# Two-layer hybrid block plus recurrent and pooling block: the SBUF offsets of the dense products' operands are changed

## The chip, the cores and the metric

The kernel runs on one core of a Trainium2 chip. The metric is the device time of one launch in microseconds (us). SBUF, the on-chip memory, has 128 partitions; a tile's "offset" below is the byte at which it begins within each partition.

## The reference

Two blocks are computed one behind the other on an activation of 512 tokens by 1024 features, in float32.

```python
for l in range(2):                       # first block, 2 layers
    h = x @ w_in[l]                      # 1024 -> 768 + 352 + 1792 columns
    mix = concat(stick_breaking(h), latent_attention(h), rwkv7(h)) @ w_o[l]
    x = layer_norm(ALPHA * x + mix)
    u_act, u_gate = split(x @ ffn_w_up[l])            # 1024 -> 2 * 2816
    hid = gelu(causal_conv3(u_act)) * u_gate
    x = layer_norm(ALPHA * x + hid @ ffn_w_down[l])   # 2816 -> 1024
for i in range(2):                       # second block: one recurrent, one pooling layer
    x = x + gate_m * mixer_i(modulate(rms_norm(x)))
    u = relu(modulate(rms_norm(x)) @ ffn_w1[i])       # 1024 -> 4096
    x = x + gate_f * ((u * u) @ ffn_w2[i])            # 4096 -> 1024
return rms_norm(x)
```

## The kernel before

Features lie on the partitions and the 512 tokens along a partition: x is [128, 8, 512], eight feature tiles of 512 floats (2048 bytes) each. A dense product is built from chunks of the weights, 128x8x128 floats (512 KB), that are streamed from HBM in the order of use. One chunk gives one output tile of 128 features by 512 tokens in one of two PSUM banks (dense0, dense1), from eight 128x128 weight blocks.

The precision of float32 is kept by splitting both operands into a high and a low part in the type float32r, which TensorE takes in one go. ScalarE copies a landed chunk of `raw` to its high part `wh` (L1345), VectorE subtracts to get the low part `wl` (L1959), and each weight block then costs three matmuls: high weights by high activations (L581), high weights by low activations (L582), low weights by high activations (L583). In all three the weight block is the stationary operand, loaded by LDWEIGHTS, and the activation tile of 512 columns is the moving one, streamed by MATMUL. A row of the trace names the moving tile first: `dense<-xh,wh` streams xh against wh.

```python
pe.matmul(o, a, h, start=first, stop=False)          # L581: wh, activation high
pe.matmul(o, a, l, start=False, stop=False)          # L582: wh, activation low
return pe.matmul(o, b, h, start=False, stop=last)    # L583: wl, activation high
```

The activation's two parts are xh and xl for the products that read x (the input, mixer, output and up projections), and hidh and hidl for the down projections of both blocks and for the recurrent layer's block-diagonal products. ScalarE writes hidh (L1684), VectorE writes hidl (L1991). The small low-rank products of the first block read the pairs latent_h/latent_l and lora_in_h/lora_in_l in the same three matmuls. In the pooling layer (L1250 to L1252) the roles are turned: the weights are moving, 256 columns of them, and xh, xl or a single column of shift_h/shift_l, repeated 128 times, is stationary; the values of the latent attention (L790 to L792) are made in the same way with latent_h and latent_l stationary. All else on TensorE is ordinary float32.

The order of work on each engine is written out by hand; SyncE (SP) issues the loads of `raw` in two slots of one chunk each, as the slots come free. The engines wait for one another by semaphores: TensorE for `lo_done` (the chunk's wl is there), for `bank_free`, and for the semaphores of its activation tiles; ScalarE's L1345 waits until TensorE is through with the chunk that was in the slot (`pe_chunk`).

SBUF is laid out by hand as well. `sb` and `Region` place one tile behind the other and round each size up to 32 bytes; the first tile begins at a multiple of 64 bytes. Everything up to and with `cst` therefore begins at a multiple of 64 bytes. The size of cst is 7944 bytes, which is rounded to 7968, and with it most of what comes behind begins 32 bytes past a multiple of 64.

Of the kernel before, what the change touches and what calls it, by code (L numbers as in the profile page):

```python
# [18 lines left out]
F32 = mybir.dt.float32  # L19
F32R = mybir.dt.float32r  # L20
# [6 lines left out]
P = 128  # L27
S = 512
D = 1024
KT = D // P  # L30
CHUNK = KT * P
BLOCKS = S // P
# [9 lines left out]
DECAY = float(np.exp(-0.5))  # L42
LN_EPS, RMS_EPS, GN_EPS = 1e-5, 1e-6, 64e-5
NEG = -1e30


C_MLA, C_SB, C_WAG = 0, 3, 9
# [84 lines left out]
VC, NVC = columns(CONSTS)  # L132
# [84 lines left out]
def build(nc, x_in, stream, mod_stream, vecs1, vecs2, consts, bands, c_rows, out):  # L217
    ctx = ExitStack()
    with ctx:

        top = [nc.sbuf_usable_end - nc.sbuf_bytes_remaining + 63]
        top[0] -= top[0] % 64
        limit = nc.sbuf_usable_end

        def at(name, shape, offset, dt=F32):
            size = 4 * int(np.prod(shape[1:]))
            assert offset + size <= limit, (name, offset, size, limit)
            return nc.alloc_sbuf_tensor_at(name, shape, dt, offset=offset)

        def sb(name, shape, dt=F32):  # L230
            t = at(name, shape, top[0], dt)
            top[0] += (4 * int(np.prod(shape[1:])) + 31) // 32 * 32
            return t

        x = sb("x", [P, KT, S])
        xh_at = top[0]
        xh = sb("xh", [P, KT, S], F32R)
        xl_at = top[0]
        xl = sb("xl", [P, KT, S], F32R)
        raw = sb("raw", [P, 2, CHUNK])  # L240
        wh = sb("wh", [P, 2, KT, P], F32R)
        wl = sb("wl", [P, 2, KT, P], F32R)
        cst = sb("cst", [P, NVC])
        pv_next = sb("pv_next", [P, NV1])
        pv = sb("pv", [P, NV1])
        one_minus = sb("one_minus", [P, 14 + 4])
        pv2 = sb("pv2", [P, NV2])
        cond = sb("cond", [P, D])
        mod = sb("mod", [P, DEPTH, 48])
        small = sb("small", [P, 16, 8])  # L250
# [16 lines left out]
        r0 = top[0]  # L267

        class Region:
# [2 lines left out]

            def __call__(self, name, shape, dt=F32):
                t = at(name, shape, self.at, dt)
                self.at += (4 * int(np.prod(shape[1:])) + 31) // 32 * 32
                return t


        rg = Region(front_at)
# [7 lines left out]
        rg = Region(r0)  # L287
# [11 lines left out]
        rg = Region(at0)  # L299
# [9 lines left out]
        rg = Region(wts_end)  # L309
# [16 lines left out]
        rg = Region(vsb_at)  # L326
# [15 lines left out]
        yy = hats[:, 1]  # L342

        rg = Region(r0)
        hidh = rg("hidh", [P, 8, S], F32R)
        hidl = rg("hidl", [P, 8, S], F32R)
        hf = rg("hf", [P, 2, S])
        ua = rg("ua", [P, S + 4])
# [7 lines left out]
        gate = at("gate", [P, 8, S], front_at)  # L356
        xc = rg("xc", [P, 8, S])
        gx_upper = rg("gx_upper", [P, 4, S])
        tb_last = rg("tb_last", [P, S])
        gx_lower = at("gx_lower", [P, 4, S], mraw_at)  # L360
        ga_lower = at("ga_lower", [P, 6, S], krv_at + 16384)
        ga_upper = at("ga_upper", [P, 2, S], krv_at + 8192)
        shift_h = rg("shift_h", [P, 8], F32R)
        shift_l = rg("shift_l", [P, 8], F32R)
        band = at("band", [P, 8, P + 16], front_at)
        z_tok = at("z_tok", [P, 4, BLOCKS, 256], r0)
        z_shift = at("z_shift", [P, 4, 256], r0 + 16384)


        ga = [ga_lower[:, m, :] for m in range(6)] + [ga_upper[:, m, :] for m in range(2)]  # L370
# [204 lines left out]
        def _(pe):  # L575
            def split_product(o, w, w_rows, k_rhs, first, last):

                (slot, cols), (h, l) = w, k_rhs
                a = wh[w_rows, slot].rearrange("p k m -> p (k m)")[:, cols:cols + P]
                b = wl[w_rows, slot].rearrange("p k m -> p (k m)")[:, cols:cols + P]  # L580
                pe.matmul(o, a, h, start=first, stop=False)  # L581
                pe.matmul(o, a, l, start=False, stop=False)  # L582
                return pe.matmul(o, b, h, start=False, stop=last)  # L583
# [196 lines left out]
            def latent_up(L, pl):  # L780

                s0, s1 = C_UP % 2, (C_UP + 1) % 2
                pe.wait_ge(lo_done, pl.chunk(C_UP) + 1)
                pe.wait_ge(cl_ready, L * 3 + 3)
                ukv_h = wh[:, s0].rearrange("p k m -> p (k m)")[:, 768:1024]
                ukv_l = wl[:, s0].rearrange("p k m -> p (k m)")[:, 768:1024]
                for tb in range(BLOCKS):
                    o = aux[tb // 2][:, 256 * (tb % 2):256 * (tb % 2) + 256]
                    th, tl = ch[:, 2, tb * P:(tb + 1) * P], cl[:, 2, tb * P:(tb + 1) * P]
                    pe.matmul(o, th, ukv_h, start=True, stop=False)  # L790
                    pe.matmul(o, th, ukv_l, start=False, stop=False)
                    m = pe.matmul(o, tl, ukv_h, start=False, stop=True)  # L792
                    if tb % 2:
                        m.then_inc(vup_pe, 1)
                for p in range(2):
                    split_product(aux[4 + p][:], (s0, 512 + p * P), slice(0, P),
                                  (ch[:, 2, :], cl[:, 2, :]), True, True).then_inc(up_pe, 1)
                for h in UP_HEADS:
                    if h == 2:
                        pe.wait_ge(vtok_ready, L * 2 + 2)  # L800
                    if h < 2:
                        pe.wait_ge(vmla_ready, L * 2 + h + 1)
                    m = split_product(aux[h][:], (s0, h * P), slice(0, P),
                                      (ch[:, 0, :], cl[:, 0, :]), True, False)
                m.then_inc(pe_chunk, 1)
                pe.wait_ge(lo_done, pl.chunk(C_UP + 1) + 1)
                for h in UP_HEADS:
                    m = split_product(aux[h][:], (s1, h * P), slice(0, 64),
                                      (ch[0:64, 1, :], cl[0:64, 1, :]), False, True)
                    m.then_inc(up_pe if h != UP_HEADS[-1] else pe_chunk, 1)  # L810
# [393 lines left out]
            for h in range(4):  # L1204
                pe.wait_ge(lo_done, pl.chunk(C_AX + h) + 1)
                pe.wait_ge(hidl_ready, H0 + 2 * h + 2)
                for o in range(4):
# [3 lines left out]
                    for k in range(2):  # L1211
                        m = split_product(aux[n % 6][:], (h % 2, (2 * o + k) * P), slice(0, P),
                                          (hidh[:, 2 * h + k, :], hidl[:, 2 * h + k, :]),
                                          k == 0, k == 1)
# [26 lines left out]

            def pool_weights(w, g, k):

                return w[:, g // 2].rearrange("p k m -> p (k m)")[
                    :, 512 * (g % 2) + 256 * k:512 * (g % 2) + 256 * k + 256]

            def token_rows(o, h, l, g, k):
# [88 lines left out]
        def _(act):  # L1336
            chain = Chain(act, act_chain)

            def prepare(pl, s, i=0, lead=False):

                slot = s % 2
                act.wait_ge(w_landed[slot], pl.landed(s, i))
                if not lead:
                    act.wait_ge(pe_chunk, pl.chunk(s, i) - 1)
                act.activation(wh[:, slot].rearrange("p k m -> p (k m)"), raw[:, slot, :],  # L1345
                               ACT.Copy).then_inc(hi_done, 1)

            def done(pl, s, i=0, more=True):
# [6 lines left out]
            def early(pl, s, q):  # L1355


                for j in range(2):
                    act.wait_ge(w_landed[j], pl.landed(s + j, 1))
                    act.wait_ge(pe_half, 2 * q + j + 1)  # L1360
                    act.activation(wh[:, j, 0:4].rearrange("p k m -> p (k m)"),
                                   raw[:, j, 0:4 * P], ACT.Copy).then_inc(hi_half, 1)

            def rest(pl, s):

                slot = s % 2
                act.wait_ge(pe_chunk, pl.chunk(s) + 1)
                act.activation(wh[:, slot, 4:8].rearrange("p k m -> p (k m)"),
                               raw[:, slot, 4 * P:8 * P], ACT.Copy).then_inc(hi_done, 1)

            def square(k, m):
# [496 lines left out]
            for i in range(4):  # L1868
                for j in range(2):
                    m = i * 2 + j  # L1870
# [80 lines left out]
        def _(dve):  # L1951
            chain = Chain(dve, dve_chain)
            tt, stt, ts = dve.tensor_tensor, dve.scalar_tensor_tensor, dve.tensor_scalar
            MUL, ADD, SUB = ALU.mult, ALU.add, ALU.subtract

            def prepare(n, slot):

                dve.wait_ge(hi_done, n + 1)
                tt(wl[:, slot].rearrange("p k m -> p (k m)"), raw[:, slot, :],  # L1959
                   wh[:, slot].rearrange("p k m -> p (k m)").bitcast(F32), SUB)\  # L1960
                    .then_inc(lo_done, 1)

            def done(pl, s, i=0, more=True):
# [5 lines left out]
            def early(q):  # L1969


                for j in range(2):
                    dve.wait_ge(hi_half, 2 * q + j + 1)
                    tt(wl[:, j, 0:4].rearrange("p k m -> p (k m)"), raw[:, j, 0:4 * P],
                       wh[:, j, 0:4].rearrange("p k m -> p (k m)").bitcast(F32), SUB)\
                        .then_inc(lo_half, 1)

            def rest(pl, s):

                slot = s % 2  # L1980
                dve.wait_ge(hi_done, pl.chunk(s, 1) + 1)
                tt(wl[:, slot, 4:8].rearrange("p k m -> p (k m)"), raw[:, slot, 4 * P:8 * P],
                   wh[:, slot, 4:8].rearrange("p k m -> p (k m)").bitcast(F32), SUB)\
                    .then_inc(lo_done, 1)

            def refill(pl, s, i=0, more=True):
# [434 lines left out]
            for L in range(DEPTH):  # L2421
# [8 lines left out]
                for a in range(4):  # L2430
                    for e in range(2):
# [4 lines left out]
                        m = 2 * a + e  # L2436
# [12 lines left out]
                for g, tiles in enumerate(GROUPS1):  # L2449
# [17 lines left out]
                    for i in range(tiles):  # L2467
                        t = L * 22 + 8 * g + i
                        m = i + 8 * g
# [131 lines left out]
            for i in range(4):  # L2601
                for j in range(2):
                    m = i * 2 + j
# [382 lines left out]
```

## Time and profile before

| | us |
|---|---|
| median of 3 runs | 2461.92 |
| lowest and highest | 2461.33, 2462.2 |
| span of the profiled execution, first to last instruction | 2460.3 |
| TensorE busy in it | 2385.6 |

The profile gives the profiled execution's span; the runs' times lie 1.0 to 1.9 us above it, which is what lies around the span. In a row of the page, busy time is in us and the mean duration of one instruction in ns. TensorE's matmuls are pipelined: one starts before the one ahead of it has ended. So the cost of one in a stream is the distance from its start to the next one's start, and not its duration, and the rows of the timeline give that distance.

### The profile page before, as it was taken

Reading aid. Unit: us, or ns where it says so; the run is one execution under the profiler, and the core shown is the slowest. Engines: PE = TensorE matmul, PEld = TensorE weight load, DVE = VectorE, ACT = ScalarE, POOL = GpSimd, SP = SyncE. Lnnn points to the kernel's source line nnn. Section 1 sums busy time; section 2 is a strip of 40 time slices with the busy share of each in tenths; the row PEclk is TensorE's granted clock in tenths of the full one; section 3 lists DMA queues with packets and bytes.
Section 4 is the critical chain, followed back from the end, with each engine's and each line's share of the span. In section 5 each row is a group of like instructions: output and inputs, shape, how many; then the busy total and the mean of one; then the engine's idle time right before and its main releaser. Section 6 shows DMA issues by size and latency. Waiting matters only on the chain.

```text
span 2460.3 us, 35763 instructions
## 1 busy us (share of the span) xinstructions
PE 2385.6 (97%) x13448; PEld 1890.4 (77%) x13448; DVE 1378.6 (56%) x1936; ACT 982.1 (40%) x1507; POOL 242.1 (10%) x192
## 2 busy tenths in 40 slices
PE   8999999999999999999999999999999999999998
PEld 6766767888887765777888887777888888788886
DVE  4547767656545447857656546575443345533443
ACT  5535435333235535534323234564232233422332
POOL 0041210000022032311000012101000001000001
PEclk9999999999999999999999998999999999999999
DMA  4210014555432210003555431222222222222222
GB/s 157 86 60 18 19 52 147 191 192 188 140 108 70 86 65 30 19 29 137 195 188 189 155 101 57 89 77 96 94 96 97 97 94 69 78 97 97 97 94 85
DMA packets 68796, 248.33 MB, mean 101 GB/s; under 512 B 7632, under 2 KB 8144, under 8 KB 68688
## 3 DMA queue, kind: packets, MB, share of 16 engines
q1 hardware_dynamic: 68688, 246.85, 29.8%
q8 instruction: 72, 1.18, 0.2%
q14 instruction: 36, 0.29, 0.0%
HBM read 244.72 MB, written 2.10 MB: 100 GB/s over the span
## 4 chain that ended last, share of the span: by engine, by line
PE 86%; DVE 7%; ACT 4%; issue 2%; DMA 0%; POOL 0%; DVEq 0%; SPq 0%; ACTq 0%; POOLq 0%
PE dense L581 24%; PE dense L583 24%; PE dense L582 24%; PE aux L688 2%; PE aux L875 1%; PE aux L845 1%; PE aux L862 1%; ACT wh L1345 1%; PE aux L953 1%; PE aux L964 1%; PE aux L1049 1%; DVE wl L1959 1%; PE aux L695 1%; PE dense L609 1%; PE aux L849 0%
## 5 line engine op out<-in xcount | busy, mean ns | idle before, releaser
L581 PE MATMUL dense<-xh,wh 128*128 128x512 f32 x1840 | 733.6, 399 | 24.7 <-DVE wl L1959 10.6
L1345 ACT ACTIVATE wh<-raw 128x1024 fp32r<-128x1024 f32 x346 | 366.9, 1060 | 960.7 <-PE dense L583 951.7
L1959 DVE TENSOR_TENSOR wl<-raw,wh 128x1024 fp32r<-128x1024 f32 x346 | 427.0, 1234 | 538.6 <-ACT wh L1345 536.9
L583 PE MATMUL dense<-xh,wl 128*128 128x512 f32 x1840 | 717.4, 390 | 0.0
L582 PE MATMUL dense<-xl,wh 128*128 128x512 f32 x1840 | 717.3, 390 | 0.0
L581 PEld LDWEIGHTS dense<-xh,wh 128*128 128x128 f32 x1840 | 345.9, 188 | 122.6 <-issue 27.8
L582 PEld LDWEIGHTS dense<-xl,wh 128*128 128x128 f32 x1840 | 346.0, 188 | 73.3 <-issue 4.4
L583 PEld LDWEIGHTS dense<-xh,wl 128*128 128x128 f32 x1840 | 345.6, 188 | 73.2
L581 PE MATMUL dense<-hidh,wh 128*128 128x512 f32 x928 | 367.9, 396 | 4.5 <-DVE hidl L1991 1.9
L583 PE MATMUL dense<-hidh,wl 128*128 128x512 f32 x928 | 367.0, 396 | 0.0
L582 PE MATMUL dense<-hidl,wh 128*128 128x512 f32 x928 | 367.0, 395 | 0.0
L581 PEld LDWEIGHTS dense<-hidh,wh 128*128 128x128 f32 x928 | 174.3, 188 | 50.4 <-DVE hidl L1991 5.7
L583 PEld LDWEIGHTS dense<-hidh,wl 128*128 128x128 f32 x928 | 174.3, 188 | 42.3
L582 PEld LDWEIGHTS dense<-hidl,wh 128*128 128x128 f32 x928 | 174.3, 188 | 41.3
L2640 DVE SCALAR_TENSOR_TENSOR x<-dense,mod,x 128x512 f32 (+1 forms) x64 | 48.1, 751 | 188.3 <-PE dense L583 188.3
L2750 POOL TENSOR_TENSOR norm_sq<-norm_sq,sq 128x512 f32<-128x512 f32 x35 | 53.3, 1524 | 737.1 <-ACT sq L1379 737.1
L2458 DVE CUSTOM_DVE_ANT_0 mraw<-mraw,cond 128x1024 f32<-128x1024 f32 x96 | 117.0, 1219 | 0.0
L1684 ACT ACTIVATE hidh<-hf 128x512 f32 (+1 forms) x108 | 68.3, 632 | 101.9 <-DVE hf L2621 94.3
L1991 DVE TENSOR_TENSOR hidl<-hf,hidh 128x512 f32 (+1 forms) x108 | 74.5, 690 | 60.3 <-ACT hidh L1684 60.3
L2749 POOL TENSOR_TENSOR norm_sum<-norm_sum,x 128x512 f32<-128x512 f32 x14 | 25.3, 1809 | 671.7 <-ACT sq L1379 671.7
L1535 ACT ACTIVATE wT<-aux 128x128 f32<-128x128 f32 (+3 forms) x64 | 28.0, 437 | 89.2 <-PE aux L862 88.9
L1379 ACT ACTIVATE sq<-x 128x512 f32<-128x512 f32 x64 | 39.9, 623 | 46.0 <-DVE x L2437 20.2
(386 smaller groups left out, 2447.4 us busy)
## 6 DMA issues: line engine op xcount, KB each, us to landing
raw<-stream SPq DMA_DIRECT2D x362, 512.0 KB, 3.5
mraw<-mod_stream SPq DMA_DIRECT2D x96, 512.0 KB, 3.9
x<-x_t SPq DMA_DIRECT2D x4, 512.0 KB, 7.1
y_t<-x SPq DMA_DIRECT2D x8, 256.0 KB, 2.2
cst<-consts SPq DMA_DIRECT2D x1, 993.0 KB, 9.5
band<-bands SPq DMA_DIRECT2D x1, 576.0 KB, 4.4
cond<-c_rows SPq DMA_DIRECT2D x1, 512.0 KB, 10.7
pv_next<-vecs SPq DMA_DIRECT2D x3, 82.5 KB, 4.3
```

The lines of the kernel that those rows point to most:

```text
L581: pe.matmul(o, a, h, start=first, stop=False)
L582: pe.matmul(o, a, l, start=False, stop=False)
L583: return pe.matmul(o, b, h, start=False, stop=last)
L688: m = pe.matmul(bank[:, at:at + SUM_COLS], src[:, t * P:(t + 1) * P], const("ones", n=SUM_COLS), start=first and t == 0, stop=last, skip_g ...
L1345: act.activation(wh[:, slot].rearrange("p k m -> p (k m)"), raw[:, slot, :], ACT.Copy).then_inc(hi_done, 1)
L1379: act.activation(sq[:, m % 2, :], x[:, m, :], ACT.Square).then_inc(sq_ready, 1)
L1684: act.activation(hidh[:, slot_i, :], hf[:, j, :], ACT.Copy).then_inc(hidh_ready, 1)
L1959: tt(wl[:, slot].rearrange("p k m -> p (k m)"), raw[:, slot, :], wh[:, slot].rearrange("p k m -> p (k m)").bitcast(F32), SUB)\
L1991: tt(dst, src, hi.bitcast(F32), SUB).then_inc(ready, 1)
L2458: dve.tensor_tensor_reduce(mraw[:, j, :], mraw[:, j, :], cond[:], 1.0, 0.0, MUL, ADD, mod_col[:, m:m + 1])\
L2640: stt(x[:, m, :], dbank[j][:], mod[:, lay, bass.ds(40 + m, 1)], x[:, m, :], MUL, ADD).then_inc(bank_free[j], 1)
L2750: pool.tensor_tensor(norm_sq[:], norm_sq[:], sq[:, m % 2, :], ALU.add)\
```

## The change

No instruction is added, removed or moved: the queue of every engine holds the same instructions with the same waits and the same shapes in the same order. What changes is where tiles lie.

- Sizes are rounded up to 64 bytes instead of 32, so every tile that is placed by these two helpers begins at a multiple of 64.
- cst goes ahead of x, and x and xh begin at a multiple of 2048.
- xl, each of the now four weight tiles (wh and wl, one tile for each slot), hidh and hidl get an offset modulo 2048 of their own.
- tb_last moves into the space of cond, which the padding takes from behind it; z_tok and z_shift follow hidh and hidl.

| tile | offset before | modulo 2048, modulo 64 | offset after | modulo 2048, modulo 64 |
|---|---|---|---|---|
| xh | 32896 | 128, 0 | 40960 | 0, 0 |
| xl | 49280 | 128, 0 | 57408 | 64, 0 |
| raw | 65664 | 128, 0 | 73792 | 64, 0 |
| wh, slot 0 and 1 | 73856, 77952 | 128, 0 | 82048, 86208 | 128 and 192, 0 |
| wl, slot 0 and 1 | 82048, 86144 | 128, 0 | 90368, 94528 | 256 and 320, 0 |
| hats, norm_sum, sq, st | 105824 and on | 1376, 32 | 106368 and on | 1920, 0 |
| hidh | 150880 | 1376, 32 | 152576 | 1024, 0 |
| hidl | 167264 | 1376, 32 | 169216 | 1280, 0 |
| latent_h, lora_in_h | 195936, 179552 | 1376, 32 | 196480, 180096 | 1920, 0 |

A tile of 512 tokens is 2048 bytes and a weight block of 128 columns 512 bytes. So in the kernel before, every activation tile of xh and xl begins at 128 modulo 2048 and every weight block at 128 modulo 512.

```diff
-            top[0] += (4 * int(np.prod(shape[1:])) + 31) // 32 * 32
+            top[0] += (4 * int(np.prod(shape[1:])) + LINE - 1) // LINE * LINE      # LINE = 64
...
+        cst = sb("cst", [P, NVC])
+        top[0] += -top[0] % ROW                                                    # ROW = 2048
         x = sb("x", [P, KT, S])
         xh = sb("xh", [P, KT, S], F32R)
+        top[0] += LINE
         xl = sb("xl", [P, KT, S], F32R)
         raw = sb("raw", [P, 2, CHUNK])
-        wh = sb("wh", [P, 2, KT, P], F32R)
-        wl = sb("wl", [P, 2, KT, P], F32R)
-        cst = sb("cst", [P, NVC])
+        wh, wl = [], []
+        for name, to in (("wh0", wh), ("wh1", wh), ("wl0", wl), ("wl1", wl)):
+            top[0] += LINE
+            to.append(sb(name, [P, KT, P], F32R))
...
         rg = Region(r0)
+        rg.at += (16 * LINE - rg.at) % ROW
+        hidh_at = rg.at
         hidh = rg("hidh", [P, 8, S], F32R)
+        rg.at += 4 * LINE
+        hidl_at = rg.at
         hidl = rg("hidl", [P, 8, S], F32R)
...
-        tb_last = rg("tb_last", [P, S])
+        tb_last = at("tb_last", [P, S], cond_at)
-        z_tok = at("z_tok", [P, 4, BLOCKS, 256], r0)
-        z_shift = at("z_shift", [P, 4, 256], r0 + 16384)
+        z_tok = at("z_tok", [P, 4, BLOCKS, 256], hidh_at)
+        z_shift = at("z_shift", [P, 4, 256], hidl_at)
...
-                a = wh[w_rows, slot].rearrange("p k m -> p (k m)")[:, cols:cols + P]
+                a = wh[slot][w_rows].rearrange("p k m -> p (k m)")[:, cols:cols + P]
```

## Rows read from the trace of the kernel before

**Rows 1.** The page: span, TensorE's busy time, its granted clock in 40 slices

```profile
span 2460.3 us, 35763 instructions
PE 2385.6 (97%) x13448; PEld 1890.4 (77%) x13448; DVE 1378.6 (56%) x1936; ACT 982.1 (40%) x1507; POOL 242.1 (10%) x192
...
PEclk9999999999999999999999998999999999999999
```

**Rows 2.** The page: the chain that ended last, shares by engine and by line

```profile
PE 86%; DVE 7%; ACT 4%; issue 2%; DMA 0%; POOL 0%; DVEq 0%; SPq 0%; ACTq 0%; POOLq 0%
PE dense L581 24%; PE dense L583 24%; PE dense L582 24%; PE aux L688 2%; PE aux L875 1%; PE aux L845 1%; PE aux L862 1%; ACT wh L1345 1%; PE aux L953 1%; PE aux L964 1%; PE aux L1049 1%; DVE wl L1959 1%; PE aux L695 1%; PE dense L609 1%; PE aux L849 0%
```

**Rows 3.** Groups by line: count | busy us, mean ns | idle before, what ended it

```profile
L581 PE MATMUL dense<-xh,wh 128*128 128x512 f32 x1840 | 733.6, 399 | 24.7 <-DVE wl L1959 10.6 <-DVE xl L2022 4.2 <-ACT ua L1715 2.4
L583 PE MATMUL dense<-xh,wl 128*128 128x512 f32 x1840 | 717.4, 390 | 0.0
L582 PE MATMUL dense<-xl,wh 128*128 128x512 f32 x1840 | 717.3, 390 | 0.0
L1959 DVE TENSOR_TENSOR wl<-raw,wh 128x1024 fp32r<-128x1024 f32 x346 | 427.0, 1234 | 538.6 <-ACT wh L1345 536.9
L581 PE MATMUL dense<-hidh,wh 128*128 128x512 f32 x928 | 367.9, 396 | 4.5 <-DVE hidl L1991 1.9 <-DVE wl L1959 1.8 <-ACT nt L1862 0.8
L583 PE MATMUL dense<-hidh,wl 128*128 128x512 f32 x928 | 367.0, 396 | 0.0
L582 PE MATMUL dense<-hidl,wh 128*128 128x512 f32 x928 | 367.0, 395 | 0.0
L1345 ACT ACTIVATE wh<-raw 128x1024 fp32r<-128x1024 f32 x346 | 366.9, 1060 | 960.7 <-PE dense L583 951.7 <-PE aux L1252 4.9 <-PE aux L583 2.9
```

**Rows 4.** Timeline, TensorE, xh and xl moving: start us, duration us, instruction

```profile
2125.25 0.39 PE L583 MATMUL dense<-xh,wl 128*128 128x512 f32 x1
...
2130.69 0.39 PE L583 MATMUL dense<-xh,wl 128*128 128x512 f32 x1
```

**Rows 5.** Timeline, TensorE, hidh and hidl moving

```profile
2150.09 0.40 PE L583 MATMUL dense<-hidh,wl 128*128 128x512 f32 x1
...
2155.69 0.40 PE L583 MATMUL dense<-hidh,wl 128*128 128x512 f32 x1
```

**Rows 6.** Timeline, pooling: a repeated column stationary, then xh and xl

```profile
2059.96 0.28 PE L1252 MATMUL aux<-wh,shift_l 128*128 128x256 f32 x1
...
2060.64 0.28 PE L1252 MATMUL aux<-wh,shift_l 128*128 128x256 f32 x1
...
2065.03 0.28 PE L1250 MATMUL aux<-wh,xh 128*128 128x256 f32 x1
...
2065.39 0.28 PE L1250 MATMUL aux<-wh,xh 128*128 128x256 f32 x1
```

**Rows 7.** Timeline, latent values: latent_h and latent_l stationary, weights moving

```profile
76.17 0.28 PE L790 MATMUL aux<-wh,latent_h 128*128 128x256 f32 x1
...
77.57 0.40 PE L581 MATMUL aux<-latent_h,wh 128*128 128x512 f32 x1
```

**Rows 8.** Timeline, plain float32: hats moving, then cst moving

```profile
319.25 0.59 PE L1143 MATMUL aux<-ysq,cst 128*128 128x512 f32 x1
319.68 1.02 PE L1136 MATMUL aux<-hats,cst 128*128 128x512 f32 x2
...
278.50 2.73 PE L1017 MATMUL aux<-cst 128*128 128x512 f32 x6
```

**Rows 9.** Busy time by stretch: stretch, length, engines, granted clock, DMA share

```profile
1700.00:2060.00 360.00, 359.38 (x1567) 291.38 (x1566) 166.33 (x185) 118.59 (x154) 13.18 (x8) 1.00 0.27 92
2140.00:2195.00 55.00, 55.00 (x238) 44.44 (x238) 20.14 (x23) 12.68 (x14) 0.00 (x0) 1.00 0.29 96
```

**Rows 10.** Waits: who waited for whom, us in total, times, longest

```profile
ACT wh L1345 <- PE dense L583: 951.7, 306, 5.0
PE dense L581 <- DVE wl L1959: 12.3, 8, 8.3
```

More of the change, by code:

```diff
@@ L44 @@
 NEG = -1e30
+LINE = 64
+ROW = 2048
 C_MLA, C_SB, C_WAG = 0, 3, 9
@@ L219, in build @@
     with ctx:
-        top = [nc.sbuf_usable_end - nc.sbuf_bytes_remaining + 63]
-        top[0] -= top[0] % 64
+        top = [nc.sbuf_usable_end - nc.sbuf_bytes_remaining + LINE - 1]
+        top[0] -= top[0] % LINE
         limit = nc.sbuf_usable_end
@@ L247, in build @@
         pv2 = sb("pv2", [P, NV2])
+        cond_at = top[0]
         cond = sb("cond", [P, D])
@@ L274, in __call__ @@
                 t = at(name, shape, self.at, dt)
-                self.at += (4 * int(np.prod(shape[1:])) + 31) // 32 * 32
+                self.at += (4 * int(np.prod(shape[1:])) + LINE - 1) // LINE * LINE
                 return t
@@ L578, in split_product @@
                 (slot, cols), (h, l) = w, k_rhs
-                a = wh[w_rows, slot].rearrange("p k m -> p (k m)")[:, cols:cols + P]
-                b = wl[w_rows, slot].rearrange("p k m -> p (k m)")[:, cols:cols + P]
+                a = wh[slot][w_rows].rearrange("p k m -> p (k m)")[:, cols:cols + P]
+                b = wl[slot][w_rows].rearrange("p k m -> p (k m)")[:, cols:cols + P]
                 pe.matmul(o, a, h, start=first, stop=False)
@@ L784, in latent_up @@
                 pe.wait_ge(cl_ready, L * 3 + 3)
-                ukv_h = wh[:, s0].rearrange("p k m -> p (k m)")[:, 768:1024]
-                ukv_l = wl[:, s0].rearrange("p k m -> p (k m)")[:, 768:1024]
+                ukv_h = wh[s0][:].rearrange("p k m -> p (k m)")[:, 768:1024]
+                ukv_l = wl[s0][:].rearrange("p k m -> p (k m)")[:, 768:1024]
                 for tb in range(BLOCKS):
@@ L1242, in pool_weights @@
             def pool_weights(w, g, k):
[L1244 removed]
+                return w[g // 2][:].rearrange("p k m -> p (k m)")[
                     :, 512 * (g % 2) + 256 * k:512 * (g % 2) + 256 * k + 256]
@@ L1344, in prepare @@
                     act.wait_ge(pe_chunk, pl.chunk(s, i) - 1)
-                act.activation(wh[:, slot].rearrange("p k m -> p (k m)"), raw[:, slot, :],
+                act.activation(wh[slot][:].rearrange("p k m -> p (k m)"), raw[:, slot, :],
                                ACT.Copy).then_inc(hi_done, 1)
@@ L1360, in early @@
                     act.wait_ge(pe_half, 2 * q + j + 1)
-                    act.activation(wh[:, j, 0:4].rearrange("p k m -> p (k m)"),
+                    act.activation(wh[j][:, 0:4].rearrange("p k m -> p (k m)"),
                                    raw[:, j, 0:4 * P], ACT.Copy).then_inc(hi_half, 1)
@@ L1367, in rest @@
                 act.wait_ge(pe_chunk, pl.chunk(s) + 1)
-                act.activation(wh[:, slot, 4:8].rearrange("p k m -> p (k m)"),
+                act.activation(wh[slot][:, 4:8].rearrange("p k m -> p (k m)"),
                                raw[:, slot, 4 * P:8 * P], ACT.Copy).then_inc(hi_done, 1)
@@ L1958, in prepare @@
                 dve.wait_ge(hi_done, n + 1)
-                tt(wl[:, slot].rearrange("p k m -> p (k m)"), raw[:, slot, :],
-                   wh[:, slot].rearrange("p k m -> p (k m)").bitcast(F32), SUB)\
+                tt(wl[slot][:].rearrange("p k m -> p (k m)"), raw[:, slot, :],
+                   wh[slot][:].rearrange("p k m -> p (k m)").bitcast(F32), SUB)\
                     .then_inc(lo_done, 1)
@@ L1973, in early @@
                     dve.wait_ge(hi_half, 2 * q + j + 1)
-                    tt(wl[:, j, 0:4].rearrange("p k m -> p (k m)"), raw[:, j, 0:4 * P],
-                       wh[:, j, 0:4].rearrange("p k m -> p (k m)").bitcast(F32), SUB)\
+                    tt(wl[j][:, 0:4].rearrange("p k m -> p (k m)"), raw[:, j, 0:4 * P],
+                       wh[j][:, 0:4].rearrange("p k m -> p (k m)").bitcast(F32), SUB)\
                         .then_inc(lo_half, 1)
@@ L1981, in rest @@
                 dve.wait_ge(hi_done, pl.chunk(s, 1) + 1)
-                tt(wl[:, slot, 4:8].rearrange("p k m -> p (k m)"), raw[:, slot, 4 * P:8 * P],
-                   wh[:, slot, 4:8].rearrange("p k m -> p (k m)").bitcast(F32), SUB)\
+                tt(wl[slot][:, 4:8].rearrange("p k m -> p (k m)"), raw[:, slot, 4 * P:8 * P],
+                   wh[slot][:, 4:8].rearrange("p k m -> p (k m)").bitcast(F32), SUB)\
                     .then_inc(lo_done, 1)
```

## Prediction

> **What bounds the kernel now.** I read the page's first part, then the chain of waits, then the groups by line, and last the timeline of TensorE alone. The first two say that TensorE is the bound: it is busy for 2385.6 of 2460.3 us at nearly full granted clock [rows 1], and it holds 86% of the chain, 72% of it in the three lines of the split product, L581 to L583 [rows 2]. The other engines have room: in the stretch from 1700 to 2060 us, which is the first feed-forward part of the second block, TensorE is busy for 359.38 of 360 us, VectorE for 166 and ScalarE for 119 [rows 9]. ScalarE's high parts of the weights wait 951.7 us in all for TensorE to free a slot, while TensorE waits for the low parts 12.3 us in all, 8 times [rows 10]. So a nanosecond off each dense matmul is a nanosecond off the kernel, and one put on is one on it, until VectorE or ScalarE becomes the bound, which is far off.
>
> The groups by line then show the one thing on which this change can act. With xh or xl moving a matmul lasts 390 ns on average (399 for L581, which bears the waits at the head of a chunk); with hidh or hidl moving it lasts 395 to 396, in all three lines, at the same shape and with the same weight tiles [rows 3]. Durations overlap, so I take the distance of starts. Over 24 matmuls of one chunk's length, xh and xl go from 2125.25 to 2130.69 us: 5.44 / 24 = 226.7 ns each [rows 4]. With hidh and hidl they go from 2150.09 to 2155.69: 5.60 / 24 = 233.3 ns each [rows 5]. The stretch around the second is one in which TensorE is busy all 55 of 55 us at granted clock 1.00 [rows 9], which is 2.4 GHz, so it is neither the clock nor a wait. The difference is 6.7 ns, 16 clock cycles, on each matmul.
>
> What distinguishes the two? xh and xl begin at 128 modulo 2048, a multiple of 64, and the weights at 128 as well. hidh and hidl begin at 1376 modulo 2048, 32 past a multiple of 64. So two things differ at once: the moving operand's alignment to 64 bytes, and the offset between moving and stationary operand, which is zero modulo 512 in the first case and not in the second. The change touches both. The whole question is which of them costs the 6.7 ns, and what the second does by itself.
>
> **The change part by part.** No instruction is added or moved, so there is no issue cost, no new wait and no queue to be moved past; every term is a change in the duration of instructions that are there.
>
> First, hidh and hidl come to a multiple of 64. I take the alignment of the moving operand for the cause. What speaks for it: in the values of the latent attention, weights (aligned, at 128) are moving and the latent tiles, 32 past a multiple of 64 and at another offset modulo 512, are stationary. These 12 matmuls of 256 columns go from 76.17 to 77.57, 116.7 ns each [rows 7]. The pooling product with equal offsets and all aligned takes 2065.39 - 2065.03 = 0.36 for 3, 120 ns each [rows 6]. So unequal offsets and an unaligned stationary operand do not cost anything there; what remains for the 6.7 ns is the moving operand. It also matters in float32r only: plain float32 with the unaligned hats moving steps by 1.02 - 0.59 = 0.43 us, and with the aligned cst moving by (2.73 - 0.59) / 5 = 0.43 us, taking 0.59 us for the last one's duration [rows 8].
> The count is 928 in each of three lines, 2784 [rows 3]. 96 more of the same kind (the block-diagonal products into aux) and 132 of the low-rank products with latent and lora tiles moving are unaligned too; I count them at the same price, as they are the same instruction. (2784 + 96 + 132) x 6.67 ns = 20.1 us. Some follow a wait or fall in a stretch at half clock, where the streaming is not the limit; I take off 3%, which gives 19.5 us. All of it lies on the path, since nothing is waited for in these stretches except 4.5 us before L581 [rows 3]. What is late next: with 227 instead of 233 ns a chunk takes 24 x 0.227 = 5.44 us, in which ScalarE has 1.06 us and VectorE 1.23 us to do for the weights [rows 3] and about one tile's work besides; the loads (512 KB in 5.44 us, where DMA is busy for 29% at 5.6 us a chunk [rows 9]) keep up. Nothing comes in its place.
>
> Second, xh, xl and the weights get unequal offsets, all still multiples of 64. This is the larger quantity: 3 x 1840 = 5520 matmuls [rows 3], 5.5 us for each nanosecond. The trace does not show such a pair, aligned and unequal, for 512 moving columns. Bounds from the nearest rows: from above, it behaves as hid did, 6.7 ns more, +36.8 us. From below, the next weights' load comes to disturb the stream less. That it does disturb shows in pooling: with a single repeated column as stationary operand six matmuls go from 2059.96 to 2060.64, 113.3 ns each, against 120 with xh and xl [rows 6], 6.7 ns less. Over all 5520 + 2784 dense matmuls that is at most -55 us. I take zero, the nearest rows being those of the kernel itself: within a chunk the weight block steps by 512 bytes modulo 2048, so it is at equal offset with the moving tile only in every fourth block and 512, 1024 or 1536 away otherwise, and the starts step by 0.22 or 0.23 us throughout the 24 of [rows 4]. An offset modulo 2048 by itself is thus already being varied and does nothing; only an offset below 512 is new.
> The Trainium skill, "TensorE: Matmul & The Clock Gate", section on what happens when a matmul is issued, says of this: "Loading the next tile's weights doesn't steal SBUF read bandwidth from the running matmul." By it the second part is worth exactly zero. The two halves of [rows 6], 120 and 113.3 ns, do not agree with it to the letter, which is why the case of a gain stays open below.
>
> Third, all other tiles come to multiples of 64: activations in hats, norm_sum, decay and the rest. Plain float32 showed no price of it [rows 8], and VectorE and ScalarE have slack. The low part of x or hid as VectorE writes it is off the path. Zero, within 2 us either way. tb_last in place of cond and the order of cst in front cost no instruction.
>
> Sum on the profiled execution: 2460.3 - 19.5 = 2440.8 us of span. The runs lie 1.0 to 1.9 us above the span, so 2442.3 us against the median of 2461.92.
>
> **The rivals.**
> A further gain: the offsets below 512 take apart the weights' loading and the streaming. For it: repeated columns save 6.7 ns, and the latent products with unequal offsets 3.3 ns against the pooling ones (116.7 to 120). Against it: the latter can come from the run of only 12 matmuls after a wait. At 3.3 ns over 8304 dense matmuls it would be 27 us more, 2415 us; at the bound of 6.7 ns 2387 us.
> Nothing: 32 bytes off is not what makes hid slow, nor does the offset below 512 matter for x; the pace is set by something that stays, such as hid's being at another place than the weights. Then 2460 to 2463 us. The Trainium skill, "SBUF — State Buffer", Specifications, speaks for this: it gives cachelines of 16 bytes, and 32 bytes past a multiple of 64 is the start of such a line, so by that page the alignment to 64 buys nothing and hid's term is zero. The 390 against 396 ns are not explained by it, and nothing in the rows shows a 16-byte line.
> Slower, one mechanism: the 6.7 ns come from an offset between moving and stationary operand that is not zero modulo 512, whatever the alignment. Before, xh, xl and all weight blocks shared 128; the change gives that up everywhere and cures nothing for hid, which still lies at 1024 and 1280 against 128 to 320. Price: 5520 x 6.67 = +36.8 us, 2499 us. It outweighs the gain of hid from 19.5 / 5520 = 3.5 ns on each x matmul. For it: in the rows both properties go together, so 512-column rows cannot exclude it. Against it: [rows 7], where unequal offsets cost nothing. If the offset costs x half of that while alignment cures hid, the sum is 2442 + 18 = 2460.
>
> **How the numbers follow.** The forecast (alignment cures hid, x stays) has 50%, 2442 us. The further gain 20%, from 2387 to 2435 us. Nothing, or a loss on x that just eats the gain, 13%. Slower 17%, from 2467 to 2499 us. A measurement of this kernel can tell some 0.2% (5 us) from no change. So faster 0.70, same 0.13, slower 0.17. For the range I leave out about a tenth below and a tenth above: from 2402 us (half-way down the further gain) to 2468 us. The likeliest case's own range is 2436 to 2448 us.
>
> **What the profile after would show.** If I am right, the groups with hidh and hidl moving fall from 396 to 390 ns and the starts in a down-projection chunk step by 227 ns; the groups with xh and xl stay at 390 and 227; VectorE's and ScalarE's groups keep their durations; TensorE's busy time falls by about 19 us and its waits stay as they are. The low-rank products with latent and lora tiles moving fall alike. If xh's groups leave 390 ns in either direction, the offset below 512 matters and my second term is wrong; if hid stays at 396 while it is a multiple of 64, the first is. If both groups come out equal but at neither 390 nor 396, the mechanism is one of the relation between the two operands and I had the cause wrong though perhaps the sign right.

## The result and the profile after

The changed kernel takes 2470.86 us (2468.01 to 2473.04, 4 runs) against 2461.62 us for the kernel before on the same chip. The ratio is 1.0046 with a 95% interval of 1.0034 to 1.0058: slower by about 9 to 11 us. I had forecast 2442 us, 0.8% faster, and the time lies outside the range.

The first rows are the page of the profiled execution after, beside [rows 1]; the groups by line behind them answer to [rows 3]. The line numbers are 11 higher.

```profile
span 2468.1 us, 35763 instructions
PE 2394.7 (97%) x13448; PEld 1890.3 (77%) x13448; DVE 1380.5 (56%) x1936; ACT 980.7 (40%) x1507; POOL 241.8 (10%) x192
```

```profile
L592 PE MATMUL dense<-xh,wh 128*128 128x512 f32 x1840 | 741.8, 403 | 23.8 <-DVE wl L1970 9.8 <-DVE xl L2033 6.0 <-ACT ua L1726 2.3
L594 PE MATMUL dense<-xh,wl 128*128 128x512 f32 x1840 | 727.3, 395 | 0.0
L593 PE MATMUL dense<-xl,wh 128*128 128x512 f32 x1840 | 721.5, 392 | 0.0
L1970 DVE TENSOR_TENSOR wl<-raw,wh 128x1024 fp32r<-128x1024 f32 x346 | 426.9, 1234 | 551.4 <-ACT wh L1356 549.5
L592 PE MATMUL dense<-hidh,wh 128*128 128x512 f32 x928 | 368.3, 397 | 4.5 <-DVE hidl L2002 1.9 <-DVE wl L1970 1.8 <-ACT nt L1873 0.8
L593 PE MATMUL dense<-hidl,wh 128*128 128x512 f32 x928 | 368.2, 397 | 0.0
L594 PE MATMUL dense<-hidh,wl 128*128 128x512 f32 x928 | 366.4, 395 | 0.0
```

The counts are the same, TensorE's waits differ by at most 2 us in a line, and VectorE's instruction for wl takes 1234 ns as before. The matmuls with hid moving did not get faster: 395 to 397 ns instead of 395 to 396. Those with xh and xl moving got slower, each of the three lines by another amount: 399 to 403, 390 to 395, 390 to 392 ns. Before, the two lines without the waits at the head of a chunk agreed (390 ns each); now they don't, and that is a first hint that a particular pair of tiles matters.

The timeline of TensorE in a chunk of each kind, to lay beside [rows 4, 5]:

```profile
1800.04 0.39 PE L594 MATMUL dense<-xh,wl 128*128 128x512 f32 x1
...
1805.54 0.39 PE L594 MATMUL dense<-xh,wl 128*128 128x512 f32 x1
...
1860.29 0.39 PE L594 MATMUL dense<-hidh,wl 128*128 128x512 f32 x1
...
1865.89 0.40 PE L594 MATMUL dense<-hidh,wl 128*128 128x512 f32 x1
```

24 steps with x moving take 5.50 us, 229.2 ns each, where it was 226.7. (Over the second block's feed-forward parts the mean step with x moving is 230.0 ns, where it was 227.0, steps with a wait left out.) With hid moving they take 5.60 us, 233.3 ns each, as before.

Where the time went by stage: the four feed-forward parts, first in the kernel before, then after (stretch | length | busy us of TensorE, its weight loads, VectorE, ScalarE, GpSimd | granted clock, DMA share, GB/s).

```profile
378.02:746.29 368.27, 364.70 (x1584) 296.78 (x1585) 220.73 (x291) 133.93 (x180) 26.33 (x19) 1.00 0.49 161
1126.81:1495.03 368.22, 364.67 (x1585) 296.75 (x1585) 220.71 (x291) 133.92 (x180) 26.27 (x19) 1.00 0.49 161
1701.97:2056.86 354.89, 354.27 (x1538) 287.68 (x1537) 163.03 (x180) 115.04 (x149) 13.18 (x8) 1.00 0.27 93
2092.66:2447.59 354.93, 354.31 (x1536) 287.65 (x1537) 149.89 (x172) 109.81 (x141) 12.64 (x8) 1.00 0.26 89
```

```profile
379.23:750.66 371.43, 368.01 (x1584) 297.38 (x1584) 220.73 (x291) 133.74 (x180) 26.34 (x19) 1.00 0.49 160
1130.10:1502.00 371.90, 368.47 (x1585) 297.46 (x1585) 220.72 (x291) 133.73 (x180) 26.33 (x19) 1.00 0.49 159
1705.79:2062.92 357.13, 356.53 (x1537) 288.32 (x1537) 163.06 (x180) 114.92 (x149) 13.17 (x8) 1.00 0.28 93
2098.48:2455.61 357.13, 356.53 (x1537) 288.34 (x1537) 149.93 (x172) 109.71 (x141) 12.61 (x8) 1.00 0.27 88
```

They lose 3.16, 3.68, 2.24 and 2.20 us, 11.3 us in all, at granted clock 1.00 in both and with TensorE busy for 99% of each or more. The rest of the span is 3.5 us shorter in this execution. That is no effect of the change that I can show: 3.4 us of it lie between the recurrent layer's start and the feed-forward part behind it, where the granted clock happened to be lower in the execution before.

```profile
1522.66:1693.30 170.64, 161.64 (x674) 127.51 (x673) 107.12 (x135) 93.61 (x135) 22.95 (x16) 0.98 0.26 86
1693.30:1701.97 8.67, 7.39 (x31) 4.73 (x30) 4.43 (x8) 5.12 (x7) 0.00 (x0) 0.80 0.23 83
```

```profile
1529.85:1697.94 168.09, 159.60 (x674) 125.44 (x673) 107.12 (x135) 93.05 (x135) 22.96 (x16) 1.00 0.27 87
1697.94:1705.79 7.85, 5.90 (x32) 3.63 (x30) 4.44 (x8) 5.11 (x7) 0.00 (x0) 1.00 0.27 90
```

### The profile page after: what moved, and what is told of

It is laid out like the page before. It is cut to its first block, busy times and chain, and to the rows that moved or that the text cites. A ratio compares the mean times of both kernels' runs of the same rounds, so it can differ in the third digit from the quotient of the medians.

```text
span 2468.1 us, 35763 instructions
## 1 busy us (share of the span) xinstructions
PE 2394.7 (97%) x13448; PEld 1890.3 (77%) x13448; DVE 1380.5 (56%) x1936; ACT 980.7 (40%) x1507; POOL 241.8 (10%) x192
## 4 chain that ended last, share of the span: by engine, by line
PE 87%; DVE 6%; ACT 4%; issue 2%; POOL 0%; DMA 0%; DVEq 0%; ACTq 0%; SPq 0%
PE dense L592 25%; PE dense L594 24%; PE dense L593 24%; PE aux L699 2%; PE aux L886 1%; PE aux L856 1%; ACT wh L1356 1%; PE aux L873 1%; DVE wl L1970 1%; PE aux L964 1%; PE aux L975 1%; PE aux L1060 1%; PE dense L620 1%; PE aux L592 0%; PE aux L706 0%
## 5 line engine op out<-in xcount | busy, mean ns | idle before, releaser
L592 PE MATMUL dense<-xh,wh 128*128 128x512 f32 x1840 | 741.8, 403 | 23.8 <-DVE wl L1970 9.8
L1970 DVE TENSOR_TENSOR wl<-raw,wh 128x1024 fp32r<-128x1024 f32 x346 | 426.9, 1234 | 551.4 <-ACT wh L1356 549.5
L594 PE MATMUL dense<-xh,wl 128*128 128x512 f32 x1840 | 727.3, 395 | 0.0
```

What stands on the lines that cost most here:

```text
L1970: tt(wl[slot][:].rearrange("p k m -> p (k m)"), raw[:, slot, :], wh[slot][:].rearrange("p k m -> p (k m)").bitcast(F32), SUB)\
```

## The experiments

Theory A says that the place of the moving tile relative to the stationary block decides the pace. Theory B says that the moving tile's alignment to 64 bytes does, as I had forecast. "Distance" is the weights' offset minus the moving tile's. Each experiment but the second and e10 starts from the changed kernel, with the eight operand tiles placed by a helper, here in the form of e1:

```diff
-        top[0] += -top[0] % ROW
...
+        def sb_at(name, shape, r):
+            top[0] += (r - top[0]) % 512
+            t = at(name, shape, top[0], F32R)
+            top[0] += 4 * int(np.prod(shape[1:]))
+            return t
+        xh = sb_at("xh", [P, KT, S], 0)
+        xl = sb_at("xl", [P, KT, S], 0)
+        wh0 = sb_at("wh0", [P, KT, P], 0)      # wl0, wh1 and wl1 alike; raw behind them
...
-        rg.at += (16 * LINE - rg.at) % ROW
+        rg.at += (0 - rg.at) % 512             # hidh, and the same ahead of hidl
```

**e1: all eight at one offset, aligned.**

> All tiles at multiples of 64 as in the changed kernel, but xh, xl, hidh, hidl and all four weight tiles at the same offset, 0 modulo 512 (the padding and the order of raw and cst differ with it). Theory A, the pace of a split-product matmul depends on the distance modulo 512 between the moving tile and the stationary block that is loaded meanwhile, and is best known at distance zero: xh, xl and hid all go at 226.7 ns, 2461.6 - 20 = 2442 us. Theory B, the 64-byte alignment of the moving tile alone sets it, and what slowed x in the changed kernel is something else in its layout, such as the operands changing offset from one instruction to the next: also 2442 us. Theory C, the other tiles' alignment or the order of tiles costs the 8 us: x at 231 and over 2465 us.

Measured: 2444.66 us, ratio to the kernel before 0.9943 (0.9930 to 0.9956). The groups by line of e1:

```profile
L601 PE MATMUL dense<-xh,wh 128*128 128x512 f32 x1840 | 734.2, 399 | 25.4 <-DVE wl L1979 10.5 <-DVE xl L2042 6.0 <-ACT ua L1735 2.4
L603 PE MATMUL dense<-xh,wl 128*128 128x512 f32 x1840 | 718.3, 390 | 0.0
...
L601 PE MATMUL dense<-hidh,wh 128*128 128x512 f32 x928 | 363.7, 392 | 4.9 <-DVE hidl L2011 2.1 <-DVE wl L1979 1.8 <-ACT nt L1882 0.8
L603 PE MATMUL dense<-hidh,wl 128*128 128x512 f32 x928 | 361.9, 390 | 0.0
```

x is back at 399 and 390 ns, and hid has come down from 396 to 390 to 392. This keeps the rounding to 64 and the four separate tiles and undoes the unequal offsets. The order of raw and the weight tiles differs too, but e4 below has e1's order with other offsets and is slow. So what slowed the changed kernel was the offsets; theory C (the other tiles' alignment, or the order of tiles) falls.

**e2: the rounding to 64 alone,** in the kernel before:

```diff
-            top[0] += (4 * int(np.prod(shape[1:])) + 31) // 32 * 32
+            top[0] += (4 * int(np.prod(shape[1:])) + 63) // 64 * 64      # in sb and in Region
```

> The kernel before with one part of the change alone: sizes rounded up to 64 bytes instead of 32. xh, xl and the weights stay at 128 modulo 512, hidh and hidl come to 0 modulo 512, so distance zero for x and 128 for hid. Theory A: x stays at 226.7 ns, hid goes at something between 226 and 237 that is not 226.7 but by chance; 2455 to 2470 us. Theory B: both at 226.7 ns, 2442 us.

Measured: 2458.14 us, ratio 0.9991 (0.9981 to 1.0002), no difference that can be told.

```profile
L581 PE MATMUL dense<-hidh,wh 128*128 128x512 f32 x928 | 367.3, 396 | 4.5 <-DVE hidl L1991 1.9 <-DVE wl L1959 1.8 <-ACT nt L1862 0.8
L583 PE MATMUL dense<-hidh,wl 128*128 128x512 f32 x928 | 366.3, 395 | 0.0
```

hidh and hidl now begin at a multiple of 64, and their matmuls still take 395 to 396 ns. Alignment cured nothing.

**e3: all at one offset, none aligned.** Every 0 in the placement of e1 becomes 32.

```diff
-        xh = sb_at("xh", [P, KT, S], 0)
+        xh = sb_at("xh", [P, KT, S], 32)       # and the other seven
```

> As e1_equal, but the eight operand tiles at 32 modulo 512, so none is a multiple of 64 and all are at distance zero. Theory A: 226.7 ns throughout, 2442 us. Theory B: 233.3 ns throughout, 2461.6 + 37 = 2499 us.

Measured: 2442.25 us, ratio 0.9929 (0.9910 to 0.9947), where theory B gave 2499.

```profile
L603 PE MATMUL dense<-xh,wl 128*128 128x512 f32 x1840 | 717.7, 390 | 0.0
...
L603 PE MATMUL dense<-hidh,wl 128*128 128x512 f32 x928 | 361.9, 390 | 0.0
```

No operand is at a multiple of 64, and all go at the best pace. Between them e2 and e3 end theory B from both sides.

**e4, e6 and e7: the pace against the distance.** The placement gives each slot's weights an offset and x and hid one each, so within a chunk every matmul has the same distance.

```diff
-        wh0 = sb_at("wh0", [P, KT, P], 0)      # offset of slot 0, slot 1, x, hid: 0, 0, 0, 0
+        wh0 = sb_at("wh0", [P, KT, P], 64)     # e4: 64, 128, 0, 320; e6: 192, 256, 0, 224; e7: 96, 160, 0, 224
```

> As e1_equal, with the weights of slot 0 at 64 and of slot 1 at 128 modulo 512, xh and xl at 0, hidh and hidl at 320. So four constant distances (weights minus moving) in one run: x 64 and 128, hid 256 and 320, all aligned to 64. Within a chunk no operand changes its offset modulo 512. Theory A: the four paces differ from one another and from 226.7 ns, between 224 and 237. Theory B: all at 226.7 ns, 2442 us.

> Constant distances (weights minus moving, modulo 512) as in e4_map_a: x 192 in slot 0 and 256 in slot 1 with xh, xl at 0; hid -32 and +32 with hidh, hidl at 224, which is 32 past a multiple of 64. If the pattern has a period of 256: x in slot 1 at about 227 to 228 ns as hid at distance 256 in e4_map_a, x in slot 0 at 229 to 234. If the period is 512: x in slot 1 at over 231. At distances of 32 either way the streams are nearly in step: between 224 and 233 ns, and this tells how narrow the good place is.

> Constant distances as in e4_map_a: x 96 and 160, hid 384 and 448 (hidh, hidl at 224 modulo 512). With a period of 256 hid at 384 goes as 128 did (232 to 233 ns) and 448 as 192; x at 96 and 160 between 231 and 234 ns.

Measured, one run each: 2480.14, 2461.32 and 2485.66 us. The times mix four distances, so the timeline is what to read: first and last of the same line in a chunk, 21 steps apart. First e6, x at distance 192 and then 256:

```profile
1734.67 0.39 PE L603 MATMUL dense<-xh,wl 128*128 128x512 f32 x1
...
1739.48 0.39 PE L603 MATMUL dense<-xh,wl 128*128 128x512 f32 x1
...
1740.16 0.39 PE L603 MATMUL dense<-xh,wl 128*128 128x512 f32 x1
...
1744.92 0.39 PE L603 MATMUL dense<-xh,wl 128*128 128x512 f32 x1
```

4.81 / 21 = 229.0 ns and 4.76 / 21 = 226.7 ns. e4, x at 128 and then at 64:

```profile
1744.47 0.40 PE L603 MATMUL dense<-xh,wl 128*128 128x512 f32 x1
...
1749.35 0.40 PE L603 MATMUL dense<-xh,wl 128*128 128x512 f32 x1
...
1750.05 0.39 PE L603 MATMUL dense<-xh,wl 128*128 128x512 f32 x1
...
1754.95 0.39 PE L603 MATMUL dense<-xh,wl 128*128 128x512 f32 x1
```

4.88 / 21 = 232.4 and 4.90 / 21 = 233.3 ns. e7, x at 96 and then hid at 448:

```profile
1754.08 0.40 PE L603 MATMUL dense<-xh,wl 128*128 128x512 f32 x1
...
1759.00 0.39 PE L603 MATMUL dense<-xh,wl 128*128 128x512 f32 x1
...
1770.88 0.39 PE L603 MATMUL dense<-hidh,wl 128*128 128x512 f32 x1
...
1775.69 0.40 PE L603 MATMUL dense<-hidh,wl 128*128 128x512 f32 x1
```

4.92 / 21 = 234.3 and 4.81 / 21 = 229.0 ns. Taken over both feed-forward parts of the second block (768 matmuls for each distance, in each the mean step of those without a wait), the traces give this table:

| distance modulo 256 | 0 | 32 | 64 | 96 | 128 | 160 | 192 | 224 |
|---|---|---|---|---|---|---|---|---|
| step ns, at this distance | 226.9 | 233.0 | 232.9 | 233.9 | 232.3 | 233.5 | 229.1 | |
| step ns, at this distance plus 256 | 227.0 (e6), 228.1 (e4) | 233.4 | 233.3 | | 232.7 | | 229.3 | 233.5 |

Distance 0 is e1's. The 233.4 at 32 plus 256 is hid in the kernel before: 128 - 1376 is 288 modulo 512. Where both rows have a value they agree: the pattern repeats after 256 bytes. Only distance 0 gives 227 to 228. Moving tiles off 64-byte alignment (hid in e6 and e7) fall into line with aligned ones.

**e5, e8 and e9: which distance counts.** A weights' load runs while the matmul before it streams (in the kernel before, L581's load starts at 2125.25 us with the matmul of L583 and takes 0.19 us), so a matmul could be hurt by its own block's distance or by that of the block loaded meanwhile.

```diff
+        xl = sb_at("xl", [P, KT, S], 128)      # e5 and e9; hidl too
+        wl0 = sb_at("wl0", [P, KT, P], 128)    # e5 and e8; wl1 too
```

> As e1_equal, but the tiles are no longer all at one offset: xh, hidh, wh at 0 and xl, hidl, wl at 128 modulo 512. The weights' load for a matmul runs while the matmul before it streams: xh streams while wh is loaded for xl, xl streams while wl is loaded for xh, xh streams while the next block's wh is loaded. So the distance between what streams and what is loaded meanwhile is zero all through, while a matmul's own two operands lie at distances 0, -128 and +128. Theory A in its sharp form (what counts is the distance to the load that runs meanwhile): 226.7 ns throughout, 2443 us. Rival A2 (the distance of a matmul's own two operands counts, or the tiles must all share one offset): L582's and L583's counterparts slow, about 232 ns in the mean of the three, 2460 to 2475 us.

Measured: 2473.21 us, ratio 1.0058 (1.0044 to 1.0072). So the sharp form of theory A is wrong: the distance to the load that runs meanwhile is zero for every matmul here, and yet the kernel is as slow as the changed one. By line the mean steps were 230, 233 and 230 ns.

> As e1_equal, but wl at 128 modulo 512; xh, xl, hidh, hidl, wh at 0. L582's counterpart has its own operands at distance 0 and runs while wl (128) is loaded; L583's has its own at 128 and runs while wh (0) is loaded; L581's has zero for both. If the load that runs meanwhile counts: L582's slows, the others stay near 227. If a matmul's own pair counts: L583's slows. If any operand of another offset spoils the step for all: all three slow, as in e5_pairs.

> As e1_equal, but xl and hidl at 128 modulo 512; xh, hidh, wh, wl at 0. By either pairing L582's counterpart alone stands at a distance (-128) and slows to about 233, the others stay near 227, mean 229, about 2460 us. If the jump of the moving operand from one matmul to the next counts, L583's or L581's slow too and the mean is 231 or more, as in e5_pairs.

Measured, one run each: 2467.18 and 2478.24 us. The timeline of e8 repeats after three matmuls:

```profile
1859.87 0.39 PE L601 MATMUL dense<-hidh,wh 128*128 128x512 f32 x1
1860.09 0.40 PE L602 MATMUL dense<-hidl,wh 128*128 128x512 f32 x1
1860.33 0.40 PE L603 MATMUL dense<-hidh,wl 128*128 128x512 f32 x1
1860.56 0.39 PE L601 MATMUL dense<-hidh,wh 128*128 128x512 f32 x1
```

Three steps take 0.69 us. In the mean of the trace L601's is 227, L602's 232 and L603's 234 ns: the matmul that runs while wl, 128 away, is loaded and the one that uses wl are both slow, the third keeps the best pace. So neither pairing alone is it. e9 goes further: only xl is elsewhere, L601 and L603 have zero distance by either pairing, and still all three are slow, 232, 231 and 232 ns. I had expected two of them at 227 and about 2460 us. I read it so that a jump of the moving operand from one matmul to the next disturbs its neighbours too; no run shows how, or rules out that a load further ahead counts.

**e10: the stationary block read from one address,** in the kernel before:

```diff
-                a = wh[w_rows, slot].rearrange("p k m -> p (k m)")[:, cols:cols + P]
+                a = wh[w_rows, slot].rearrange("p k m -> p (k m)")[:, cols:cols + 1]
+                a = a.to_broadcast([a.shape[0], P])      # b alike from wl
```

> The kernel before, in which L581 to L583 take the first column of each weight block, repeated 128 times, as stationary operand (the products of the weights' other columns are left out). The weights' load then reads one address instead of walking along 512 bytes; everything else, the offsets too, is as before. If the pace is set by the load and the stream meeting in the memory: x and hid come to one pace, near 220 ns (113.3 ns at 256 columns was 16 cycles over the columns), 2459 - 5520 x 6.7 ns - 2784 x 13.3 ns = 2385 us. If it is set by the moving operand's own address: x stays at 226.7 or falls, and hid stays 6.7 ns above it.

Measured: 2468.87 us, ratio 1.0040 (1.0024 to 1.0055), against 2385 us expected. A plain miss. Here are 27 steps with hid moving:

```profile
1859.61 0.40 PE L584 MATMUL dense<-hidl,wh 128*128 128x512 f32 x1
...
1865.86 0.39 PE L584 MATMUL dense<-hidl,wh 128*128 128x512 f32 x1
```

6.25 / 27 = 231.5 ns, down from 233.3; with x moving the mean step is 230.6, up from 226.7. The two kinds nearly meet, so the way in which the stationary block is read does set the pace, as theory A has it. But a load that stays at one address is not harmless; it is worse than one that walks in step with the stream. The gain of the repeated column in [rows 6], 113.3 against 120 ns, does not carry over to 512 columns.

**e11 and e12: the versions that beat both.** e11 puts cst, x, hats and all that follows them at the same offset modulo 256 too:

```diff
+        top[0] += (128 - top[0]) % 256         # ahead of x, and ahead of front_at
+        xh = sb_at("xh", [P, KT, S], 128)      # all eight, modulo 256
```

> As e1_equal, and beyond it every large tile (x, cst, the weights, xh, xl, raw, hats, latent_h, lora_in_h, hidh, hidl) at 128 modulo 256, so the low-rank products and the plain float32 ones run at distance zero too. Theory A with a period of 256: the 8304 dense matmuls at 226.7 ns, the 132 low-rank ones 6 ns less, together 2443 us less 1 us. If plain float32 matmuls respond to the distance as well, another 2 to 5 us less.

Measured: 2441.58 us, ratio 0.9929 (0.9916 to 0.9943). It overlaps e1, so the time shows no effect of the low-rank or the plain float32 products. The trace does show one for the low-rank products. Here is the same stretch of the first layer's, in the kernel before and in e11:

```profile
78.74 0.40 PE L583 MATMUL aux<-latent_h,wl 128*128 128x512 f32 x1
...
81.54 0.40 PE L583 MATMUL aux<-latent_h,wl 128*128 128x512 f32 x1
```

```profile
79.36 0.39 PE L605 MATMUL aux<-latent_h,wl 128*128 128x512 f32 x1
...
82.08 0.39 PE L605 MATMUL aux<-latent_h,wl 128*128 128x512 f32 x1
```

2.80 / 12 = 233.3 ns before, 2.72 / 12 = 226.7 ns in e11, where latent_h and latent_l have the weights' offset modulo 256. The first five steps of this run, just behind another kind of product, take 229 to 236 ns in e11, and most of the other low-rank runs are broken by waits; in the mean of all their steps without a wait it is 230 ns against 233. 132 matmuls at 3 ns are 0.4 us, too little for the times to tell.

e12 gives tiles different offsets modulo 512 again, but in steps of 256:

```diff
+        xl = sb_at("xl", [P, KT, S], 256)      # wh1, wl0 and hidh too; xh, wh0, wl1 and hidl at 0
```

> As e1_equal, but with tiles at offsets of their own modulo 512 again, in steps of 256 instead of 64: xh, wh of slot 0, wl of slot 1 and hidl at 0, xl, wh of slot 1, wl of slot 0 and hidh at 256. If only the offset modulo 256 counts, in mixed order too: 226.7 ns throughout and the time of e1_equal, 2443 us. If all must agree modulo 512 or more: some three quarters of the matmuls stand at another offset than their neighbours, as in e5_pairs, 231 ns and 2470 us.

Measured: 2440.75 us, ratio 0.9928 (0.9915 to 0.9942).

```profile
L602 PE MATMUL dense<-xl,wh 128*128 128x512 f32 x1840 | 717.8, 390 | 0.0
...
L602 PE MATMUL dense<-hidl,wh 128*128 128x512 f32 x928 | 362.0, 390 | 0.0
```

390 ns in both, in mixed order. What must agree is the offset modulo 256 and nothing above it. e5 (tiles 128 apart) is 1.3% slower than e12 (tiles 256 apart) by their ratios, at the same instructions; which tiles are set apart differs between the two.

## Why the prediction was wrong

The bound was read rightly. TensorE is the bound, each nanosecond of a dense matmul arrives in the time, nothing else moved, and 19.5 us was about the right price for hid's excess: e3, e11 and e12, which remove it, gain about 17.5 us by their ratios, and e1 14.

The step that failed is the first term, "I take the alignment of the moving operand for the cause". I had written that alignment and equality of offsets go together in the 512-column rows [rows 3 to 5], and then chose between them by the 12 matmuls of [rows 7]. These have 256 columns, with the weights moving and the activation stationary, and I took them to speak for 512 columns with the roles the other way. They don't: what they show is true of their own shape, where the sign is the opposite. The pooling product has that shape too, and the changed kernel gives it unequal offsets. Here are 21 steps of it there, to lay beside the 120 ns of [rows 6]:

```profile
2071.73 0.28 PE L1261 MATMUL dense<-wh,xh 128*128 128x256 f32 x1
...
2074.16 0.28 PE L1261 MATMUL dense<-wh,xh 128*128 128x256 f32 x1
```

2.43 / 21 = 115.7 ns. Over the 96 pooling matmuls with xh or xl stationary the mean step without waits is 116.5 ns here, and 119.7 to 119.9 in the kernel before, e1, e2, e3, e10, e11 and e12, whose x and weights share an offset modulo 256; in e4 to e9 it is 117.7 to 119.1. So in the pooling product, at 256 columns, unequal offsets are faster; in the dense products, at 512, they are slower. It is not a rule for every distance: the latent values take 116.8 ns in the mean in the kernel before, but 120.4 in e2, with latent_h 128 away from the weights. Whether the number of columns or the exchanged roles turns the sign, no run separates. The changed kernel has hidh and hidl at 0 modulo 256, wh at 128 and 192 and wl at 0 and 64, so five of six of hid's matmuls stand at distances of 128, 192 or 64, and its 233 ns stayed: 0 us in place of -19.5.

The second term, zero for x, failed too. I argued that within a chunk the weight block steps by 512 modulo 2048 without effect [rows 4]. That observation was right and is just what a period of 256 demands; the conclusion that only an offset below 512 was new was right as well. I then took zero for it instead of the bound from hid's rows. The four feed-forward parts hold 3648 of the 5520 x matmuls and lost 11.3 us, hid's pace being the same: 3.1 ns each. That lies inside my bounds (-6.7 to +6.7) and not at 6.7, and some of the new pairs do stand at 0 or 192 modulo 256, where the step is 227 or 229 ns. In so mixed an order I have no rule that adds the pairs up: by the table they would average about 231 ns for x and a little less for hid, and the mean steps are 230.0 and 233.3.

Of the rivals, the slower one had the mechanism: unequal offsets cost, whatever the alignment, and alignment cures nothing. I gave it 17%. Its price was too high (6.7 ns on each x matmul, where the feed-forward parts lost 3.1; 36.8 us, where the kernel lost 9 to 11), and its modulus of 512 should be 256. The rival of a further gain rested on the 256-column rows; their 3.3 ns were real, for that shape alone. The page of the Trainium skill "SBUF — State Buffer", Specifications, with its cachelines of 16 bytes, would have had alignment to 64 buy nothing, and on that point e2 and e3 agree with it (0.9991, and 390 ns at 32 past a multiple of 64). The sentence from the Trainium skill, "TensorE: Matmul & The Clock Gate", section on what happens when a matmul is issued, by which loading the next tile's weights takes no SBUF read bandwidth from the running matmul, would have had the weights' place cost nothing. For these float32r products it does cost: where the weights lie moves the step from 227 to 234 ns. Whether read bandwidth is what is lost, no run shows.

What stays open is the mechanism below the 256 bytes. Why 227 ns at distance 0, when 512 clock cycles at 2.4 GHz are 213.3 ns; why 256 columns with the weights moving go the other way; why 192 is milder than the rest; and what slows all three matmuls in e9, where only one has a tile elsewhere. Finer distances than 32 bytes were not tried.

## What to carry to other kernels

For float32r matmuls of 512 moving columns whose stationary block changes with every matmul, place every moving and every stationary tile at the same offset modulo 256 bytes; here that is worth 0.7% of a kernel bound by TensorE, for a few bytes of padding. For 256 columns with the weights moving, measure before you do: here equal offsets cost them 1 to 3 ns a matmul. When two properties go together in every steady row of a trace, let the test be a kernel that separates them in the same shape: rows of another shape, here half the columns and exchanged roles, won't do. And spreading offsets "so that nothing collides" is not a safe default; streams that run in step may want to start in step.

## What the runs showed of the hardware that I had not expected

The step of a 128x128 by 512-column float32r matmul depends on the operands' places in SBUF with a period of 256 bytes: 227 ns at equal offset, 229 at 192, 232 to 234 at the other multiples of 32. With 256 columns and the weights moving it is the other way round in the pooling product: 120 ns at equal offset, 116.5 in the changed kernel. Alignment to 64 bytes has no part in it. A stationary operand read from one address is slower (230.6 ns with x) than one of 512 bytes that starts in step (226.7).
